# Feed-forward blocks that begin with k outermost over three weight units, on one core

## The chip, the cores and the metric

The kernel runs on one core of a Trainium2 chip. Its engines are TensorE (matrix products; PE, with its weight loads as PEld), VectorE (DVE), ScalarE (ACT) and SyncE (SP), which here only issues DMA transfers. GpSimd (POOL) does next to nothing. The metric is the device time of the one core in microseconds (us), lower is better. Times come from three runs; where time goes is read from one profiled execution.

## The reference

Two stacks of transformer layers work on one sequence of 256 tokens of width 1024, in float32. The first stack (2 layers) mixes with differential attention, SSD and GLA side by side; the second (4 layers) with stick-breaking, MoBA, sliding-window and again stick-breaking attention, each under a modulation (`ada`) by a condition vector. What the change touches is the feed-forward block that closes each of the six layers, and the end of the mixer ahead of it:

```python
# stack 1, layer i
h = h + mix @ w_out[i]
f = rms_norm(h, ffn_norm[i])
h = h + (jax.nn.silu(f @ w_ffn_gate[i]) * (f @ w_ffn_up[i])) @ w_ffn_down[i]

# stack 2, layer i
mod = c_act @ ada_w[i] + ada_b[i]
sh1, sc1, g1, sh2, sc2, g2 = [m[:, None, :] for m in jnp.split(mod, 6, axis=-1)]
...
x = x + g1 * y                                   # y: the attention's output
h = modulate(rms_norm_2(x, norm_gain[i, 1]), sh2, sc2)
x = x + g2 * swiglu(h, ffn_w_gate[i], ffn_w_up[i], ffn_w_down[i])
```

The hidden width of the feed-forward block is 2816.

## The kernel before, in words

**Layout.** x and h lie transposed in on-chip memory: 8 tiles of 128 features (k-tiles) by 256 tokens. All weights stream from memory once, in units of 128 x 1024 numbers (512 KB), one unit per buffer of `wslot`, slots 0 to 10. The attention phases use slots 0 to 3 (q, k, v, out projection), the GLA and SSD phases slots 0 to 7, the feed-forward blocks slots 8 (gate), 9 (up) and 10 (down), and slots 4 to 7 for the weights of a modulation table.

**Split products.** To keep float32 accuracy at the fast product rate, a weight unit is split in two: ScalarE copies it rounded into `w_hi` (helpers `mix_high` and `high`), VectorE writes the rest into `w_lo` (helpers `low_of` and `low`), and only then is the slot free for the next load. `w_hi` and `w_lo` have five parts; the attention uses parts 0, 1 and 4. h is split in the same way into `h_hi` and `h_lo`. A product is three matmuls (`three`: hi x hi, hi x lo, lo x hi) of 128 x 128 weights by 256 tokens, lines 575, 576 and 577 in turn.

**The phases.** `schedule` writes a list of phases: norm, attention (`att`), `ssd`, `gla`, `add`, `ffn` and so on. Every engine walks the same list in its own instruction stream, and the streams meet only at semaphores; `schedule` counts for each semaphore how often it has risen when a phase begins. Each engine does its instructions strictly in the order of the program.

**The feed-forward block (`ffn`).** It has 22 chunks (NF) of 128 hidden features. For one chunk TensorE does `up` (8 k-tiles of gate, then 8 of up: 48 matmuls into one bank), ScalarE silu, VectorE the product `mid`, both split mid, and TensorE does `down` (24 matmuls into `acc`). The order on TensorE is up(0), up(1), down(0), up(2), down(1) and so on, so that the elementwise work of a chunk lies under the next chunk's `up`. In one chunk's step VectorE does: the two `w_lo` of the next chunk, mid, the `w_lo` of down, mid_lo, and then, where the block carries a modulation table (`ada`), two `ada_unit` of two operations each. Four of the six blocks carry one: both of stack 1, and the first two of stack 2.

**Its beginning.** SP issues the loads of chunk 0's gate and up in the norm phase; slots 8 and 9 are free by then, so these go out as soon as SP gets there, behind the last out-projection unit of the attention. ScalarE splits them at the head of the norm phase, ahead of the squares, and VectorE ahead of its wait for `rstd`. After `rstd` VectorE makes the scaled tiles and, two tiles behind, `h_lo` (`h_low`), ScalarE `h_hi` between; the semaphore `h_parts` counts finished k-tiles. TensorE's `up(0, 0, first=True)` waits for `h_parts` ahead of each k-tile of gate. Chunk 1's units go through slots 8 and 9 too, after chunk 0's have been split.

**The last head of an attention phase.** `whole` is one step of the attention loop: on ScalarE and VectorE it handles pair of heads `i` and ends `prior = i - 1`. While there are more pairs, ScalarE (lines 1087 to 1091) and VectorE (`next_low`, line 1326) also split the q and k units of the next pair; in the last pair (`more` false) they don't. In stick-breaking attention `next_low` stands ahead of VectorE's reading of the scores (line 1353), in the others behind `qk_ready` and ahead of the same reading (line 1383).

## Time and profile before

| | us |
|---|---|
| median of 3 runs | 2578.78 |
| lowest, highest | 2577.83, 2583.71 |
| span of the profiled execution | 2580.4 |

The profiled execution's span, from its first instruction to its last, is 1.6 us above the median of the runs; nothing of note lies around it. The profile page gives busy time per engine, the groups of instructions by source line, and each group's mean duration. The trace behind it gives single instructions with their start, their duration, how long their engine had been idle before them and what ended that (in brackets), the chain of waits that leads to the last instruction, the busy time and the granted TensorE clock of any stretch (1.00 is 2.4 GHz, 0.50 is 1.2 GHz), and for each DMA the time from issue to landing. All starts are in us from the span's start. A matmul's own duration includes its way through the array; what counts for throughput is the distance from one start to the next.

### The profile page before, as it was taken

How to read it: one execution, taken by the hardware profiler on the slowest of the kernel's cores; microseconds unless marked ns; L12 is line 12 of the kernel's file. 1: busy time of each engine (PE TensorE's matmuls, PEld its weight loads, DVE VectorE, ACT ScalarE, POOL GpSimd, SP SyncE). 2: the span in 40 equal slices, each digit the busy share in tenths (PEclk: the TensorE clock that was granted, in tenths of full speed). 3: DMA queues.
4: the chain of work that ended last, by engine and by line, in shares of the span. 5: the costliest groups of instructions: out<-in, count | busy, mean ns of one | idle time of the engine just before them, and what ended most of it. 6: DMA issues, size and time to landing. Idle time of an engine off the chain costs nothing.

```text
span 2580.4 us, 44727 instructions
## 1 busy us (share of the span) xinstructions
PE 2369.4 (92%) x17136; PEld 2203.8 (85%) x17136; DVE 1498.5 (58%) x2564; ACT 1021.1 (40%) x1670; POOL 0.2 (0%) x4
## 2 busy tenths in 40 slices
PE   5799899988798899989899999899978899998998
PEld 4687699987686799979899978799966799897998
DVE  4433177745441477836677776577766554666544
ACT  3312244414231344325544444444444544455443
POOL 0000000000000000000000000000000000000000
PEclk8898799998898899999899999899989899998999
DMA  4343179962433299844289854299842366442664
GB/s 127 91 112 102 33 251 289 290 192 83 123 83 99 77 291 292 271 127 129 85 273 291 289 165 127 86 292 286 276 114 82 115 181 185 127 132 85 194 186 131
DMA packets 553295, 436.26 MB, mean 169 GB/s; under 512 B 31824, under 2 KB 479352, under 8 KB 553080
## 3 DMA queue, kind: packets, MB, share of 16 engines
q1 hardware_dynamic: 549840, 431.35, 55.2%
q10 hardware_dynamic: 3368, 3.71, 0.5%
q8 instruction: 59, 0.97, 0.2%
q14 instruction: 28, 0.23, 0.0%
HBM read 433.96 MB, written 1.05 MB: 169 GB/s over the span
## 4 chain that ended last, share of the span: by engine, by line
PE 85%; DVE 7%; ACT 3%; issue 1%; DMA 1%; DVEq 1%; ACTq 1%; SPq 0%
PE bank L575 12%; PE bank L576 12%; PE bank L577 12%; PE acc L575 6%; PE acc L576 6%; PE acc L577 6%; PE bank L561 5%; PE bank L702 5%; PE acc L620 3%; PE bank L980 2%; PE bank L779 2%; PE bank L585 1%; PE bank L570 1%; PE bank L691 1%; PE bank L745 1%
## 5 line engine op out<-in xcount | busy, mean ns | idle before, releaser
L575 PE MATMUL bank<-h_hi,w_hi 128*128 128x256 f32 x2704 | 787.4, 291 | 28.1 <-DVE h_lo L1251 16.1
L576 PE MATMUL bank<-h_lo,w_hi 128*128 128x256 f32 x2704 | 774.6, 286 | 0.0
L577 PE MATMUL bank<-h_hi,w_lo 128*128 128x256 f32 x2704 | 774.1, 286 | 0.0
L1013 ACT ACTIVATE w_hi<-wslot 128x1024 fp32r<-128x1024 f32 x510 | 529.8, 1054 | 527.9 <-PE acc L577 312.6
L1429 DVE TENSOR_TENSOR w_lo<-wslot,w_hi 128x1024 fp32r<-128x1024 f32 x396 | 473.2, 1221 | 263.0 <-ACT w_hi L1013 262.8
L575 PEld LDWEIGHTS bank<-h_hi,w_hi 128*128 128x128 f32 x2704 | 527.9, 195 | 46.9 <-issue 31.9
L576 PEld LDWEIGHTS bank<-h_lo,w_hi 128*128 128x128 f32 x2704 | 529.9, 196 | 0.0
L577 PEld LDWEIGHTS bank<-h_hi,w_lo 128*128 128x128 f32 x2704 | 528.8, 196 | 0.0
L575 PE MATMUL acc<-mid_hi,w_hi 128*128 128x256 f32 x1056 | 302.2, 286 | 0.5 <-DVE mid_lo L1662 0.5
L577 PE MATMUL acc<-mid_hi,w_lo 128*128 128x256 f32 x1056 | 298.7, 283 | 0.0
L576 PE MATMUL acc<-mid_lo,w_hi 128*128 128x256 f32 x1056 | 298.7, 283 | 0.0
L1251 DVE SCALAR_TENSOR_TENSOR head_work<-wslot,c_act,head_work 128x512 f32<-128x512 f32 x288 | 216.5, 752 | 24.0
L575 PEld LDWEIGHTS acc<-mid_hi,w_hi 128*128 128x128 f32 x1056 | 202.4, 192 | 0.8 <-DVE w_lo L1429 0.8
L576 PEld LDWEIGHTS acc<-mid_lo,w_hi 128*128 128x128 f32 x1056 | 202.6, 192 | 0.0
L577 PEld LDWEIGHTS acc<-mid_hi,w_lo 128*128 128x128 f32 x1056 | 202.4, 192 | 0.0
L1269 DVE TENSOR_TENSOR w_lo<-wslot,w_hi 128x1024 fp32r<-128x1024 f32 x114 | 136.2, 1220 | 49.8 <-ACT w_hi L1013 49.6
L561 PE MATMUL bank<-hT,wslot 128*128 128x256 f32 x640 | 143.1, 381 | 0.6 <-DVE sqT L1551 0.5
L702 PEld LDWEIGHTS bank<-wslot,hT 128*128 128x128 f32 x1088 | 129.2, 194 | 9.1 <-issue 9.1
L561 PEld LDWEIGHTS bank<-hT,wslot 128*128 128x128 f32 x640 | 120.9, 191 | 18.3 <-issue 1.5
L702 PE MATMUL bank<-wslot,hT 128*128 128x128 f32 x1088 | 136.2, 279 | 0.0
L575 PE MATMUL acc<-y_hi,w_hi 128*128 128x256 f32 x320 | 107.0, 334 | 21.1 <-DVE y_lo L1314 21.1
L1220 ACT ACTIVATE silu_g<-bank 128x256 f32<-128x256 f32 x132 | 49.7, 377 | 137.5 <-PE bank L577 137.3
(255 smaller groups left out, 2742.9 us busy)
## 6 DMA issues: line engine op xcount, KB each, us to landing
wslot<-in_ada_w_dram SPq DMA_DIRECT2D x192, 512.0 KB, 5.8
wslot<-in_ffn_w_gate_dram SPq DMA_DIRECT2D x88, 512.0 KB, 4.7
wslot<-in_ffn_w_up_dram SPq DMA_DIRECT2D x88, 512.0 KB, 5.4
wslot<-in_ffn_w_down_dram SPq DMA_DIRECT2D x88, 512.0 KB, 3.4
wslot<-in_w_in_dram SPq DMA_DIRECT2D x72, 512.0 KB, 4.0
wslot<-in_sb_w_in_dram SPq DMA_DIRECT2D x48, 512.0 KB, 4.5
wslot<-in_w_ffn_gate_dram SPq DMA_DIRECT2D x44, 512.0 KB, 4.9
wslot<-in_w_ffn_up_dram SPq DMA_DIRECT2D x44, 512.0 KB, 5.6
```

The costliest lines, as they stand in the source:

```text
L561: mm = pe.matmul(dst, wk(n, k), hT[:, k, :], start=(k == 0), stop=(k == KT - 1))
L575: pe.matmul(dst, w_hi[:, w, cols], hi, start=start, stop=False, skip_group_check=True)
L576: pe.matmul(dst, w_hi[:, w, cols], lo, start=False, stop=False, skip_group_check=True)
L577: return pe.matmul(dst, w_lo[:, w, cols], hi, start=False, stop=stop, skip_group_check=True)
L620: mm = pe.matmul(acc[:, m, :], wk(n, m), y, start=False, stop=False, skip_group_check=True)
L702: mm = pe.matmul(B(1, 256 + P * t, 384 + P * t), hT[:, k, P * t:P * t + P], wk(2, k), start=(k == 0), stop=(k == KT - 1))
L779: mm = pe.matmul(B(0, 0, 256), C("ones"), sqT[:, k, :], start=(k == 0), stop=(k == KT - 1))
L980: mm = pe.matmul(B(2 * b, 0, 256), wk(s, k), xT[:, k, :], start=(k == 0), stop=(k == KT - 1))
L1013: return act.activation(dst, src, ACT.Copy)
L1251: return dve.scalar_tensor_tensor(out=out, in0=x, scalar=scalar, in1=y, op0=op0, op1=op1)
L1269: dve.tensor_tensor(w_lo[:, part, :], wslot[:, n, :], w_hi[:, part, :], ALU.subtract)\
L1429: dve.tensor_tensor(w_lo[:, part, :], wslot[:, n, :], w_hi[:, part, :], ALU.subtract).then_inc(slot_used[n], 1)
```

## The change

**Loads.** The first unit of gate and up (slots 8 and 9) is no longer loaded in the norm phase but at the end of the phase ahead of it: in the second `gla` group of stack 1, and in the last pair of an attention phase of stack 2 (`first_units`). With them goes the gate unit of chunk 1, through slot 0. The up unit of chunk 1 goes through slot 1, from the norm phase. Chunk 2 is then the first one to be loaded into slots 8 and 9 in the block itself.

**Splits.** Three units (gate 0 to part 0, up 0 to part 1, gate 1 to part 2) are split in the phase ahead: in the last pair of heads, gate 0 and up 0 take the place where the next pair's q and k would be split, and gate 1 follows the last out-projection unit. In GLA all three stand at the phase's end. The norm phase splits one unit, up 1, into part 3. The first chunk's step in the block has no split of a next chunk any more. The differential attention of stack 1 is as it was.

**Products.** `first_two` does chunks 0 and 1: for each k-tile, once `h_parts` has it, the three matmuls of gate 0, up 0 and gate 1; then the 24 of up 1. `two_chunks(0, None)` no longer does `up(1)`. The same 96 matmuls are done in another order.

The core of the diff:

```diff
@@ schedule
         if split == "ffn":
-            counts.update(w_high=2, **slots(SLOT_FF, [1, 1]))
+            counts.update(w_high=1, **slots(SLOT_MIX + 1, [1]))
...
@@ SP
+            def first_units(stack, l, used, mix_used):
+
+                wg, wu, _ = ffn_weights(stack, l)
+                for n, w in enumerate((wg, wu)):
+                    load(SLOT_FF + n, mix_slot(SLOT_FF + n), unit(w, KT, 0), used[n] + 1)
+                load(0, mix_slot(0), unit(wg, KT, P), mix_used + 1)
...
                 if kind == "norm" and ph["split"] == "ffn":
-                    for n, w in enumerate(ffn_weights(ph)[:2]):
-                        load(SLOT_FF + n, mix_slot(SLOT_FF + n), unit(w, KT, 0), u[SLOT_FF + n] + 1)
+                    _, wu, _ = ffn_weights(ph["stack"], ph["layer"])
+                    load(1, mix_slot(1), unit(wu, KT, P), u[1] + 1)
...
                         if not more:
                             load(3, wslot[:, 3, :], wo[P * lo:P * lo + P, :], lo + u[3] + 1)
+                            if ph["att"] != "da":
+                                first_units(2, ph["layer"], u[SLOT_FF:SLOT_FF + 2], u[0] + ph["n"])
@@ TensorE
+                    def first_two():
+
+                        for s in (SLOT_FF, SLOT_FF + 1, 0):
+                            pe.wait_ge(slot_used[s], g(f"slot{s}") + 1)
+                        for k in range(KT):
+                            pe.wait_ge(sem["h_parts"], g("h_parts") - KT + k + 1)
+                            up_part(0, 0, k, k == 0)
+                            mm = up_part(0, 1, k, False)
+                            if k == KT - 1:
+                                mm.then_inc(sem["up_done"], 1)
+                            up_part(1, 0, k, k == 0)
+                        pe.wait_ge(slot_used[1], g("slot1") + 1)
+                        for k in range(KT):
+                            mm = up_part(1, 1, k, k == 0)
                         mm.then_inc(sem["up_done"], 1)
@@ ScalarE, attention
                         mix_high(0, 0, mix_full(0, i + 1))
                         if new_kv:
                             mix_high(1, 1, mix_full(1, ki + 1))
+                    elif i is not None and att != "da":
+                        for c in range(2):
+                            high(SLOT_FF + c, c, 16 * (g(f"slot{SLOT_FF + c}") + 1))
...
                     mix_high(3, PART_DOWN, mix_full(3, i))
+                    if not more and att != "da":
+                        high(0, 2, mix_full(0, ph["n"]))
@@ ScalarE, norm
                     if ph["split"] == "ffn":
-                        for n in range(2):
-                            high(SLOT_FF + n, n, 16 * (g(f"slot{SLOT_FF + n}") + 1))
+                        high(1, 3, 16 * (g("slot1") + g("extra1") + 1))
@@ VectorE, attention
                     def next_low():
+                        if not more:
+                            for c in range(2 if att != "da" else 0):
+                                low(SLOT_FF + c, c, g("w_high") + c + 1)
+                            return
...
                         mix_low(3, PART_DOWN, prior)
+                        if i is None and att != "da":
+                            low(0, 2, g("w_high") + 3)
...
                     if att == "sb":
-                        if more:
-                            next_low()
+                        next_low()
@@ VectorE, gla
+                    if gr:
+                        for n, part in ((SLOT_FF, 0), (SLOT_FF + 1, 1), (0, 2)):
+                            low(n, part, g("w_high") + part + 1)
```

What it moves, at the places that matter. The line numbers of the two kernels differ: 1013, 1269, 1429 and 1353 before are 1054, 1318, 1324 and 1412 after.

VectorE, the last pair of heads of the first stick-breaking layer, before. The scores are read in the second row.

```order
L1314 TENSOR_TENSOR y_lo<-bank,y_hi 128x256 [waits y_high]
L1353 TENSOR_SCALAR head_work<-bank 128x384 [waits scores] x2
L1356 TENSOR_SCALAR sm<-head_work 128x384 x2
L1360 TENSOR_TENSOR sm<-sm,pr 128x384 [waits sb_log]
```

After:

```order
L1368 TENSOR_TENSOR y_lo<-bank,y_hi 128x256 [waits y_high]
L1324 TENSOR_TENSOR w_lo<-wslot,w_hi 128x1024 [waits w_high] x2
L1412 TENSOR_SCALAR head_work<-bank 128x384 [waits scores] x2
L1415 TENSOR_SCALAR sm<-head_work 128x384 x2
L1419 TENSOR_TENSOR sm<-sm,pr 128x384 [waits sb_log]
```

Two subtractions now stand ahead of the reading, and each waits for ScalarE's `w_high`.

VectorE at the start of the first feed-forward block of stack 2, from the last pieces of h_lo to the split of chunk 2's units, before:

```order
L1251 SCALAR_TENSOR_TENSOR h_lo<-sqT,mod,h_hi 128x256 [waits h_high] x3
L1429 TENSOR_TENSOR w_lo<-wslot,w_hi 128x1024 [waits w_high] x2
L1659 TENSOR_TENSOR mid<-silu_g,bank 128x256 [waits silu_ready]
L1429 TENSOR_TENSOR w_lo<-wslot,w_hi 128x1024 [waits w_high]
L1662 TENSOR_TENSOR mid_lo<-mid,mid_hi 128x256 [waits mid_high]
L1412 TENSOR_SCALAR head_work<-wslot,c_act 128x512 [waits slot_full4]
```

After, to the same point and on to the split of chunk 2:

```order
L1300 SCALAR_TENSOR_TENSOR h_lo<-sqT,mod,h_hi 128x256 [waits h_high] x3
L1714 TENSOR_TENSOR mid<-silu_g,bank 128x256 [waits silu_ready]
L1324 TENSOR_TENSOR w_lo<-wslot,w_hi 128x1024 [waits w_high]
L1717 TENSOR_TENSOR mid_lo<-mid,mid_hi 128x256 [waits mid_high]
L1470 TENSOR_SCALAR head_work<-wslot,c_act 128x512 [waits slot_full4]
L1300 SCALAR_TENSOR_TENSOR head_work<-wslot,c_act,head_work 128x512
L1300 SCALAR_TENSOR_TENSOR head_work<-wslot,c_act,head_work 128x512 [waits slot_full5]
L1300 SCALAR_TENSOR_TENSOR head_work<-wslot,c_act,head_work 128x512
L1324 TENSOR_TENSOR w_lo<-wslot,w_hi 128x1024 [waits w_high] x2
```

Chunk 1's pair of subtractions is gone from between h_lo and mid; chunk 2's pair stays behind the ada work.

SP at the end of the first stick-breaking layer, after: the second to fourth of these loads are the first units, and the loads behind them follow without a wait for work that is still to be done.

```order
L425 DMA wslot<-in_sb_w_out_dram 128x1024 [waits slot_used3]
L425 DMA wslot<-in_ffn_w_gate_dram 128x8x128 [waits slot_used8]
L425 DMA wslot<-in_ffn_w_up_dram 128x8x128 [waits slot_used9]
L425 DMA wslot<-in_ffn_w_gate_dram 128x8x128 [waits slot_used0]
L425 DMA wslot<-in_ffn_w_up_dram 128x8x128 [waits slot_used1]
L425 DMA wslot<-in_ffn_w_down_dram 128x1024 [waits slot_used10]
L425 DMA wslot<-in_ada_w_dram 128x2x512 [waits slot_used4]
```

Before, this list went from the third row straight to a wait for slot 8, which VectorE frees in the norm phase.

## Rows read from the trace of the kernel before

**Rows 1.** The page: busy us, share, count; a group's count, busy, mean ns

```profile
PE 2369.4 (92%) x17136; PEld 2203.8 (85%) x17136; DVE 1498.5 (58%) x2564; ACT 1021.1 (40%) x1670; POOL 0.2 (0%) x4
...
L1013 ACT ACTIVATE w_hi<-wslot 128x1024 fp32r<-128x1024 f32 x510 | 529.8, 1054 | 527.9 <-PE acc L577 312.6
```

**Rows 2.** Chain of waits: start us, us to the next, what; three places

```profile
1284.97 0.21 PE acc L577
...
1294.99 0.40 DVE h_lo L1251
1295.38 0.40 DVE sqT L1251
...
1302.01 0.12 PE bank L576
```

**Rows 3.** Stretches of block starts: start:end, us, PE busy (matmuls), PEclk, DMA share, GB/s

```profile
333.09:346.47 13.38, 13.38 (x96) 0.88 0.77 249
886.50:901.01 14.51, 14.51 (x96) 0.79 0.75 234
1295.53:1309.29 13.76, 13.68 (x96) 0.88 0.73 235
1668.82:1683.19 14.37, 13.91 (x96) 0.88 0.63 212
...
sum 84.14, PE 83.07; mean PE 13.84
```

**Rows 4.** TensorE in order of time: first product of two blocks [idle before <-releaser]

```profile
1295.53 0.55 PE L575 MATMUL bank<-h_hi,w_hi 128*128 128x256 f32 x1 [1.88 <-DVE h_lo L1251]
...
1668.82 0.35 PE L575 MATMUL bank<-h_hi,w_hi 128*128 128x256 f32 x1 [1.89 <-DVE h_lo L1251]
```

**Rows 5.** Last heads of the first stick-breaking layer, VectorE and ScalarE in order of time

```profile
1271.96 1.02 DVE L1353 TENSOR_SCALAR head_work<-bank 128x384 f32<-128x384 f32 x2 [4.80 <-PE bank L657]
1272.55 0.52 ACT L1023 ACTIVATE pr<-head_work 128x384 f32<-128x384 f32 x1 [3.87 <-DVE head_work L1353]
...
1281.44 1.22 DVE L1269 TENSOR_TENSOR w_lo<-wslot,w_hi 128x1024 fp32r<-128x1024 f32 x1
...
1283.63 0.42 DVE L1314 TENSOR_TENSOR y_lo<-bank,y_hi 128x256 fp32r<-128x256 f32 x1 [0.97 <-ACT y_hi L1013]
```

**Rows 6.** First chunk of stack 2's first block: silu, mid_lo, chunk 2's gate split

```profile
1303.73 0.38 ACT L1220 ACTIVATE silu_g<-bank 128x256 f32<-128x256 f32 x1 [0.92 <-PE bank L577]
...
1306.23 0.42 DVE L1662 TENSOR_TENSOR mid_lo<-mid,mid_hi 128x256 fp32r<-128x256 f32 x1
...
1309.66 1.22 DVE L1429 TENSOR_TENSOR w_lo<-wslot,w_hi 128x1024 fp32r<-128x1024 f32 x1
```

**Rows 7.** Issue of up 0; landing us of up loads at 1267.33, 1292.44, 2386.29; all of wslot

```profile
1267.33 0.58 SPq L416 DMA_DIRECT2D wslot<-in_ffn_w_up_dram  x1
...
wslot<-in_ffn_w_up_dram SPq DMA_DIRECT2D x1, 512.0 KB, 6.1
...
wslot<-in_ffn_w_up_dram SPq DMA_DIRECT2D x1, 512.0 KB, 5.6
...
wslot<-in_ffn_w_up_dram SPq DMA_DIRECT2D x1, 512.0 KB, 4.9
...
DMA to landing us min/median/max: 3.2/5.0/15.7
```

**Rows 8.** Sliding-window layer, last heads: issue of up 0, VectorE's first reading of scores

```profile
1994.30 0.58 SPq L416 DMA_DIRECT2D wslot<-in_ffn_w_up_dram  x1
...
2000.69 0.56 DVE L1251 SCALAR_TENSOR_TENSOR sm<-bank,const 128x384 f32<-128x384 f32 x1 [2.69 <-PE bank L660]
```

**Rows 9.** MoBA layer, last heads: the same two

```profile
1633.40 0.58 SPq L416 DMA_DIRECT2D wslot<-in_ffn_w_up_dram  x1
...
1642.74 0.56 DVE L1251 SCALAR_TENSOR_TENSOR sm<-bank,const 128x384 f32<-128x384 f32 x1 [2.24 <-PE bank L660]
```

**Rows 10.** First stack, VectorE at the end of GLA, in order of time

```profile
324.29 0.69 DVE L1642 TENSOR_TENSOR xT<-xT,acc 128x512 f32<-128x512 f32 x1 [7.51 <-PE acc L620]
```

## What I predict, and how

> **What bounds the kernel now.** I read the page first: TensorE is busy for 92% of the span [rows 1]. So the time is the sum of TensorE's products and of the places where TensorE has none. Inside a feed-forward block, past its start, nothing else counts: products follow each other every 0.12 us at the full clock, and every 0.21 us at half of it [rows 2]. What is left to win or lose lies at two joints, and they are where the change works.
>
> The first is the start of the six feed-forward blocks. There h arrives from VectorE in eight k-tiles, one each 0.79 us (a 0.40 us piece of h_lo, then 0.40 us of scaling) [rows 2], and TensorE has three products per tile, 0.36 us of work at the full clock. From a block's first product to the first one of its down projection (96 products, chunks 0 and 1) the six take 84.14 us together, 13.38 to 14.51 each [rows 3]; the two that have no row there repeat rows that have one (the third stack-2 block 14.36, clock 0.88, like the second; the fourth 13.76, like the first). At 0.12 us a product 96 would need 11.5. TensorE stood idle 1.88 us ahead of such a start, waiting for h_lo [rows 4].
>
> The second joint is the end of an attention phase of stack 2. The last head's scores leave TensorE with nothing, and the chain runs over VectorE and ScalarE: in the first stick-breaking layer VectorE waits 4.80 us for the scores, and starts the moment they are there; ScalarE waits 3.87 us for VectorE [rows 5]. These holes look free, but each ends exactly when the chain goes on.
>
> **Part 1, k outermost: a gain.** With three units ready, each k-tile feeds nine products, 1.08 us at the full clock against a tile each 0.79 us. TensorE waits for the first tile only. Chunks 0 and 1 then need 96 x 0.12 + 0.13 (the first product's extra) = 11.65 us. While the granted clock is at its half level a product takes 0.213 us, so h us of half clock cost h x (1 - 0.12/0.213) = 0.44 h. Before, the granted means of 0.88 and 0.79 stand for (1 - mean) x 2 x length = 3.2, 6.1, 3.3, 3.45, 3.45 and 3.3 us at 1.2 GHz [rows 3]. In the first and third of these TensorE had been idle before the start and the half stretch began with it; I keep 3.2 and 3.3 (the fourth of stack 2 likewise), and cut the second one's 6.1 to 3.2, since TensorE was underfed through it. In the second and third block of stack 2 the first product ran at the full level (0.35 us against 0.55 [rows 4]) and the clock fell only during the trickle; with no trickle I take no half stretch there. Sum after: 2 x 13.05 + 2 x 13.1 + 2 x 11.65 = 75.6, a gain of **8.6 us**. Bounds: half stretches as long as before, 79.9 (gain 4.3); none, 69.9 (gain 14.2).
>
> The rule of the Trainium skill for this is in "TensorE: Matmul & The Clock Gate", section "HAM oscillation — how this bites in real kernels": run all k-tiles on end rather than wait between them, so that the array stays at its full clock. Taken at its word it gives the 14.2, the second rival below; the rows say that the idle ahead of the start is left as it is.
>
> **Part 2, the start's other end: a new stop.** Before, when chunk 0's gate and up were done, TensorE still had chunk 1's 48 products (5.76 us) to cover silu, mid and the split of down. Now 27 are left (3.24 us). From the start of silu to the end of mid_lo it took 1306.65 - 1303.73 = 2.92 us [rows 6]: just covered, I give 0.1 us a block, 0.5 in all (0 to 1). But in the four blocks with a modulation table to sum (both of stack 1, the first two of stack 2) VectorE then works through two ada units and only afterwards through chunk 2's gate split, whose first half ended at 1310.88, 7.15 us after silu's start [rows 6]. TensorE gets there after 3.24 - 0.2 + 24 x 0.12 = 5.9 us. It stops 7.2 - 5.9 = **1.3 us**, four times: 5.2 us. (The lower bound is 0.6 each, if ScalarE's earlier split lets VectorE close up, the upper 1.6.) After that a chunk has its 72 products again, 8.64 us, in which VectorE kept up before; it makes the debt good over the next chunks. In the two blocks without ada the split comes at once and costs nothing.
>
> **Part 3, the splits in the attention tails: a loss.** In the last head ScalarE now splits gate 0 and up 0 between copying v and the log chain, and VectorE subtracts both ahead of reading the scores. Both queues run in order, so the scores wait behind them, and they wait for the transfers. Those are issued where they were: up 0 at 1267.33, landing 6.1 us later [rows 7], 1273.43. ScalarE 1.05 [rows 1], VectorE 1.22 [rows 5], hand-overs 0.1: 1275.8 against 1271.96 [rows 5], 3.8 us. Before, nothing was behind up 0 in the DMA queue; now there are six more loads. An up load with others right behind took 5.6 us, one without 4.9 [rows 7], so up to 0.7 comes on top; I take 0.4, 4.2 us. At the tail's end VectorE also subtracts unit 2 (1.22) in a gap of 0.97 [rows 5]: 0.25. Two stick-breaking layers: **8.9 us** (8.2 to 9.6).
>
> The sliding-window layer: up 0 issued at 1994.30 [rows 8], the same 6.1: 2000.4, through both engines 2002.8, against scores read at 2000.69 [rows 8]: 2.1, with the 0.4 **2.5** (2.1 to 2.8). MoBA: VectorE's hole is 2.24 us [rows 9], the two subtractions take 2.44, and its transfers, issued 9.3 us ahead of the read (1633.40 against 1642.74), have landed by then: 0.2, with ScalarE's third split 0.3 (0.1 to 0.5). In stack 1 the three splits stand in GLA's tail, where VectorE has 7.51 us idle under the 32 products of the out projection [rows 10]; three times 1.22 is 3.7: nothing. If that cover were gone it would be 3.7 twice.
>
> Gone from the norm: a w_hi/w_lo pair on each engine, and one more pair in the first chunk. VectorE waited for rstd after them, 0; the loads that SP now issues early free nothing that anyone waits for, 0.
>
> **Sum.** -8.6 + 5.2 + 0.5 + 8.9 + 2.5 + 0.3 = **+8.8 us**. The profiled execution (span 2580.4) would become 2589.2; against the median of the runs, 2578.8, that is **2587.6**. Ends: -14.2 + 2.4 + 0 + 10.4 = -1.4, and -4.3 + 6.4 + 1 + 12.9 = +16.0.
>
> **Rivals.**
> The splits fit into the hole (not slower). Price: the tails fall from 11.7 to 0.8, 2576.7. It decides at one point: up 0 must have landed by 1271.96 - 1.22 - 1.05 - 0.1 = 1269.6, 2.3 us after its issue. The shortest landing of any load into wslot is 3.2 [rows 7]. For it: the hole itself is wider (4.80) than the work (2.44).
> The clock stays full in all six starts: 5.6 more, 2582.0. Against it: four of six starts began at half clock, after an idle that stays.
> VectorE catches up before TensorE asks for chunk 2: no 5.2, 2582.4. Against it: its order ada, then split is unchanged.
> All that is open goes badly (loads slowed by those behind, half clock as before): 2594.8.
>
> **Chances.** Forecast 0.50, fit 0.08, full clock 0.14, no stop 0.08, badly 0.13, others 0.07. A measurement of this kernel tells about 0.2%, 5.2 us, from no change. Slower: 0.44 of the forecast, all of "badly", 0.06 of the rest: 0.63. Within: 0.06, 0.04, 0.11, 0.06, 0.02: 0.29. Faster: 0.08, from the fit with a fuller clock and from what I don't see. The range for 8 in 10 takes the full clock and nearly all of the bad case, and leaves the fit: 2577.5 to 2594.
>
> **What would show it.** In the trace after: the six stretches from first product to first down product sum to some 76 us, with 96 products each and no wait for h_lo but the first; in four of them a TensorE idle of 1.3 us "w_lo" ahead of chunk 2; at the end of the stick-breaking layers a VectorE wait for ScalarE's w_hi, and of ScalarE for the DMA of ffn_w_up, with the scores read 4 us late; 2.5 us in sliding-window, next to none in MoBA and none in GLA. It is wrong if the scores are read on time, or if the clock turns out to be worth more than its 5.6 us: in the tails, above all, where it falls too and where I leave it at zero net.

## The result, and the profile after

| | before | changed |
|---|---|---|
| median, us | 2578.78 (5 runs) | 2589.59 (5 runs) |
| lowest, highest | 2577.26, 2583.71 | 2587.98, 2598.20 |
| span of the profiled execution | 2580.4 | 2587.7 |
| ratio, 95% interval | | 1.0046 [1.0027, 1.0065] |

The changed kernel is slower by 0.46%, some 12 us by the ratio. Its run of 2589.59 us has a span of 2587.7, so a run's time is its span and 1.9 us more. The profiled execution of before was then one of about 2582.3 us, in the upper part of the runs, and not 1.6 us above their median as I wrote ahead.

**The six starts.** From first product to first down product, as in [rows 3] (start:end, length, TensorE's busy time and matmuls, granted clock, DMA share, GB/s):

```profile
331.14:345.46 14.32, 14.31 (x96) 0.79 0.00 1
884.11:898.43 14.32, 14.32 (x97) 0.79 0.00 1
1300.29:1313.22 12.93, 12.93 (x97) 0.89 0.00 1
1673.30:1684.91 11.61, 11.61 (x96) 1.00 0.01 1
2031.48:2043.10 11.62, 11.62 (x97) 1.00 0.00 0
2385.50:2398.51 13.01, 13.01 (x96) 0.88 0.00 0
sum 77.81, PE 77.80; mean PE 12.97
```

Busy time equals length: TensorE no longer waits for h after the first tile. The MoBA and the sliding-window block run at the full clock and take 11.6 us, as worked out. Both stack-1 blocks have 0.79, that is 6.1 us at 1.2 GHz. The DMA share, 0.45 to 0.77 before, is nothing: those loads went out earlier.

**The stop ahead of chunk 2**, first block of stack 2, VectorE and then TensorE in order of time [idle before <-releaser]:

```profile
1310.56 0.42 DVE L1714 TENSOR_TENSOR mid<-silu_g,bank 128x256 f32<-128x256 f32 x1 [5.67 <-ACT silu_g L1269]
1311.51 1.23 DVE L1324 TENSOR_TENSOR w_lo<-wslot,w_hi 128x1024 fp32r<-128x1024 f32 x1 [0.52 <-ACT w_hi L1054]
...
1313.73 2.42 DVE L1300 SCALAR_TENSOR_TENSOR head_work<-wslot,c_act,head_work 128x512 f32<-128x512 f32 x3
1316.07 2.35 DVE L1324 TENSOR_TENSOR w_lo<-wslot,w_hi 128x1024 fp32r<-128x1024 f32 x2
```

```profile
1317.34 0.39 PE L597 MATMUL bank<-h_hi,w_hi 128*128 128x256 f32 x1 [1.02 <-DVE w_lo L1324]
```

The ada work (head_work) stands ahead of chunk 2's splits, and TensorE waits for the first of them. From the first down product (1313.22) to this row it takes 4.12 us, in all four blocks with a modulation table; before, it took 2.88 in every block. From here to their last product the four blocks take 184.9, 184.5, 184.5 and 184.5 us, against 184.4 before: the stop is paid once, and neither grows nor shrinks.

**The tail of the first stick-breaking layer**, the counterpart of [rows 5], VectorE:

```profile
1267.46 0.42 DVE L1368 TENSOR_TENSOR y_lo<-bank,y_hi 128x256 fp32r<-128x256 f32 x1 [0.29 <-ACT y_hi L1054]
1273.40 1.23 DVE L1324 TENSOR_TENSOR w_lo<-wslot,w_hi 128x1024 fp32r<-128x1024 f32 x1 [5.52 <-ACT w_hi L1054]
1275.75 1.22 DVE L1324 TENSOR_TENSOR w_lo<-wslot,w_hi 128x1024 fp32r<-128x1024 f32 x1 [1.12 <-ACT w_hi L1054]
1276.89 1.01 DVE L1412 TENSOR_SCALAR head_work<-bank 128x384 f32<-128x384 f32 x2
```

ScalarE beside it:

```profile
1272.31 1.06 ACT L1054 ACTIVATE w_hi<-wslot 128x1024 fp32r<-128x1024 f32 x1 [2.90 <-DMA wslot<-in_ffn_w_gate_dram]
1274.66 1.06 ACT L1054 ACTIVATE w_hi<-wslot 128x1024 fp32r<-128x1024 f32 x1 [1.29 <-DMA wslot<-in_ffn_w_up_dram]
```

SP's issue of up 0, and the landing of that transfer (last number, us):

```profile
1268.07 0.58 SPq L425 DMA_DIRECT2D wslot<-in_ffn_w_up_dram  x1
```

```profile
wslot<-in_ffn_w_up_dram SPq DMA_DIRECT2D x1, 512.0 KB, 6.6
```

The chain reads as one: up 0 is issued at 1268.07 and lands some 6.6 us later, ScalarE starts on it at 1274.66, VectorE follows at 1275.75, and only then, at 1276.89, reads scores that had long been there (no wait stands on that row). In [rows 5] the same reading waited for TensorE alone. It now comes 9.43 us after the y_lo ahead of it. In the trace of before that y_lo started at 1266.73, which makes 5.23:

```profile
1266.73 0.42 DVE L1314 TENSOR_TENSOR y_lo<-bank,y_hi 128x256 fp32r<-128x256 f32 x1 [0.30 <-ACT y_hi L1013]
```

In the sliding-window layer the two subtractions come at 2000.65 and 2002.97, and the scores are read at 2004.19, 6.99 us after y_lo at 1997.20, where it was 4.55:

```profile
2002.97 1.23 DVE L1324 TENSOR_TENSOR w_lo<-wslot,w_hi 128x1024 fp32r<-128x1024 f32 x1 [1.10 <-ACT w_hi L1054]
...
2004.19 0.55 DVE L1300 SCALAR_TENSOR_TENSOR sm<-bank,const 128x384 f32<-128x384 f32 x1
```

### The profile page after: what moved, and what is told of

Same layout as the page of the kernel before. It is cut to its first block, busy times and chain, and to the rows that moved or that the text cites. A ratio compares the mean times of both kernels' runs of the same rounds, so it can differ in the third digit from the quotient of the medians.

```text
span 2587.7 us, 44670 instructions
## 1 busy us (share of the span) xinstructions
PE 2360.2 (91%) x17136; PEld 2197.3 (85%) x17136; DVE 1496.9 (58%) x2564; ACT 1020.9 (39%) x1670; POOL 0.2 (0%) x4
## 4 chain that ended last, share of the span: by engine, by line
PE 82%; DVE 8%; ACT 4%; DMA 2%; DVEq 1%; issue 1%; ACTq 1%; SPq 0%
PE bank L597 12%; PE bank L598 12%; PE bank L599 12%; PE acc L597 6%; PE acc L598 6%; PE acc L599 6%; PE bank L583 5%; PE bank L724 4%; PE acc L642 3%; PE bank L1021 2%; PE bank L801 2%; PE bank L607 1%; PE bank L592 1%; DVE head_work L1300 1%; DVE w_lo L1324 1%
## 5 line engine op out<-in xcount | busy, mean ns | idle before, releaser
L1054 ACT ACTIVATE w_hi<-wslot 128x1024 fp32r<-128x1024 f32 x510 | 529.9, 1054 | 529.1 <-PE acc L599 314.0
```

The costliest lines, as they stand in the source:

```text
L1054: return act.activation(dst, src, ACT.Copy)
```

## The experiments

All are timed against runs of the kernel before on the same chip, and the ratios are taken that way. The theory: three terms make the result, a gain at the starts (k outermost), a stop ahead of chunk 2 (ada work first), and late scores in the tails (splits that wait for transfers). The rivals: the stop only moves debt that comes back later; the tails are late for another reason than the transfers; two units would have been enough.

**Chunk 2's splits first.** In the first chunk's step VectorE splits chunk 2's units ahead of the ada units, not behind (`next_pair` makes the same two `low` calls).

```diff
-                        if more and not first:
-                            for n, what in enumerate(("gate", "up")):
-                                low(SLOT_FF + n, 2 * (1 - b) + n, count + split_index(what, f + 1))
...
+                        if more and not second and not first:
+                            next_pair(f, b)
...
+                        if first:
+                            next_pair(1, 1)
                         if ada is not None:
```

> The changed kernel, with one thing moved: in the first chunk's step of a feed-forward block VectorE subtracts chunk 2's gate and up units ahead of the two ada units, not behind them. Theory (TensorE's stop ahead of chunk 2 is VectorE's order): the 4.12 us from the first down product to chunk 2's first product in the four ada blocks falls to 2.9, 5.0 us less in all, 2584.6 against the changed kernel's 2589.6. Rival (VectorE has too much to do in these blocks, and the wait comes back one chunk later): 2589.6.

Measured: 2585.59 us, ratio 1.0027 [1.0016, 1.0038].

```profile
1306.12 2.35 DVE L1324 TENSOR_TENSOR w_lo<-wslot,w_hi 128x1024 fp32r<-128x1024 f32 x2
1308.57 0.49 DVE L1470 TENSOR_SCALAR head_work<-wslot,c_act 128x512 f32<-128x512 f32 x1
```

The splits now come first. The distance from first down product to chunk 2 falls from 4.12 to 2.95 us in all four blocks, and the rest of each block keeps its length (184.4 to 184.7 us). So the stop is the order on VectorE, and no debt is behind it.

**Loads first.** The changed kernel, with SP's loads of gate 0 and up 0 at the start of the attention phase of stack 2, where slots 8 and 9 have long been free. The splits stay.

```diff
+                    if ph["att"] != "da":
+                        first_pair(2, ph["layer"], u[SLOT_FF:SLOT_FF + 2])
...
-                                first_units(2, ph["layer"], u[SLOT_FF:SLOT_FF + 2], u[0] + ph["n"])
+                                third_unit(2, ph["layer"], u[0] + ph["n"])
```

> The changed kernel, with one thing moved: in the attention phases of stack 2 SP issues the loads of gate 0 and up 0 at the phase's start, where slots 8 and 9 are free already, and not behind the last out-projection unit. The splits stay in the last pair of heads. Theory (the tails lose to transfers that two in-order queues wait for): VectorE's 2.44 us of subtractions fit into its hole of 4.80, the scores of both stick-breaking layers are read 4 us earlier, those of sliding-window 2.4, in all some 10.5 us less: 2579. Rival (it is the splits' own work on both engines that delays the chain, wherever the data are): 2589, with the scores read as late as now.

Measured: 2584.32 us, ratio 1.0011 [1.0001, 1.0021]. The same tail, VectorE:

```profile
1269.37 0.43 DVE L1373 TENSOR_TENSOR y_lo<-bank,y_hi 128x256 fp32r<-128x256 f32 x1 [0.30 <-ACT y_hi L1059]
1272.30 2.36 DVE L1329 TENSOR_TENSOR w_lo<-wslot,w_hi 128x1024 fp32r<-128x1024 f32 x2 [2.50 <-ACT w_hi L1059]
1274.63 1.02 DVE L1417 TENSOR_SCALAR head_work<-bank 128x384 f32<-128x384 f32 x2
```

The same two subtractions, in the same place, now fit into the hole: the scores are read 5.26 us after y_lo, against 5.23 before the change. The splits were never the loss; the transfers they waited for were. In the sliding-window layer the scores are read 5.77 us after y_lo here and 4.55 in the version with both repairs, as before the change; VectorE then waits for TensorE, not for a split. The ratio falls by 0.0035, some 9 us of the 10.5 expected, and such a difference is known to about 0.002.

**Both.**

> Both edits together, the split of chunk 2 ahead of the ada units and the early loads. Theory: the two stops are apart in time and add up, 15.5 us less than the changed kernel, 2574, that is 0.2% faster than the kernel before; what is left of the change is k outermost's 6.3 us, less 0.8 in the tails. Rival (one stop stands for the other, or the clock takes the gain back): 2579 or more.

Measured: 2576.26 us, ratio 0.9990 [0.9981, 0.9999]. The starts:

```profile
330.95:343.97 13.02, 13.02 (x97) 0.88 0.00 1
884.38:898.69 14.31, 14.31 (x96) 0.79 0.00 1
...
2021.33:2035.51 14.18, 14.18 (x96) 0.79 0.00 0
...
sum 79.15, PE 79.15; mean PE 13.19
```

With both repairs the change is worth a little, 0.1%, at the edge of what can be told. Of the 8.6 us forecast for the starts 5.0 remain in this trace. The sliding-window block, at the full clock in the trace of the changed kernel, is at half clock for 5.8 us here, with nothing changed at its start.

**Two units.** The kernel before, with k outermost over gate 0 and up 0 alone; loads, splits and tails as before.

```diff
-                    up(0, 0, first=True)
...
+                    for k in range(KT):
+                        pe.wait_ge(sem["h_parts"], g("h_parts") - KT + k + 1)
+                        for n in range(2):
+                            mm = three(B(0, 256 * n, 256 * n + 256), n, k_cols(k), h_hi[:, k, :], h_lo[:, k, :],
+                                       k == 0 and n == 0, k == KT - 1)
+                    mm.then_inc(sem["up_done"], 1)
```

> The kernel before, with k outermost over two units only: chunk 0's gate and up, six products for each k-tile. Loads and splits as before. Theory (a third unit is needed, since chunk 1's split comes late): TensorE is through with chunk 0 by 6.1 us after its first product, but VectorE has gate 1's split at 7.6, so it stops 1.5 us, and first product to first down product takes 13.4 us a block; in all 3 us less than before, 2576. Rival (two units do as well, 11.9 us a block): 2567.

Measured: 2580.43 us, ratio 1.0006 [0.9994, 1.0018].

```profile
1660.98:1674.48 13.50, 12.14 (x96) 1.00 0.64 213
2019.47:2032.98 13.51, 12.14 (x96) 1.00 0.42 133
...
sum 83.32, PE 80.35; mean PE 13.39
```

At the full clock 13.50 us, as expected (13.4), of which TensorE is busy 12.14. Six products per tile, 0.72 us, don't quite cover the 0.79 that a tile takes, which costs 0.5 us. The rest is one stop, between chunk 0 and chunk 1, for VectorE's split of gate 1:

```profile
1668.62 0.39 PE L575 MATMUL bank<-h_hi,w_hi 128*128 128x256 f32 x1 [1.36 <-DVE w_lo L1436]
```

It has no cost in the tails, and no gain that can be told: the 2576 us expected did not come. The third unit, split ahead of the block, is what makes the start dense.

**The old order of products** in the changed kernel: its loads and splits stay, gate 0, up 0, gate 1 and up 1 are done one after the other.

```diff
                             up_part(0, 0, k, k == 0)
-                            mm = up_part(0, 1, k, False)
-                            if k == KT - 1:
-                                mm.then_inc(sem["up_done"], 1)
+                        for k in range(KT):
+                            mm = up_part(0, 1, k, k == 0)
+                        mm.then_inc(sem["up_done"], 1)
+                        for k in range(KT):
                             up_part(1, 0, k, k == 0)
```

> The changed kernel with its early loads and splits kept and only the products put back in the old order: gate 0 (which takes the eight waits for a part of h), up 0, gate 1, up 1, each over its own eight k. Theory: k outermost gave 6.3 us over the six starts and took 5.0 us back as the stop ahead of chunk 2, since it ends chunks 0 and 1 some 2 us sooner and leaves VectorE as much less time for the splits of chunk 2. So without it the six stretches grow by 6.3 us together (towards 14.0 each at a mixed clock), the stop falls from 4.12 to 2.9 us, and the sum is the changed kernel plus 1.3 us: 2590.9 us. Rival: the stop hangs on the update units on VectorE alone and stays with the old order; then both are paid, and the time is 2589.6 + 6.3 = 2595.9 us. Second rival: the six stretches keep their gain from the early splits alone, and the time is 2589.6 - 5.0 = 2584.6 us.

Measured: 2593.36 us, ratio 1.0052 [1.0032, 1.0072].

```profile
334.10:348.60 14.50, 14.50 (x96) 0.79 0.13 45
...
1676.24:1690.59 14.35, 13.90 (x96) 0.88 0.13 45
...
sum 84.89, PE 84.14; mean PE 14.02
```

The starts are back at 84.9 us, and the distance ahead of chunk 2 at 2.88 in all six blocks. So k outermost and the stop come together, and the trace shows how. VectorE ends chunk 2's first split 7.14 us after silu's start in every block with a table, whatever the order of products. What changes is when silu starts: chunk 0's sums are complete after 48 of the 96 products in the old order and after 69 with k outermost, so silu starts 5.56 us ahead of the first down product in the old order, here and in the kernel before, and 3.07 us ahead of it in the changed kernel. Against the changed kernel's two ratios the product order is worth nothing to 0.0006 (1.3 to 3.8 us by the medians), which these runs can't tell from nothing. What is left, 0.5% over the kernel before, are the tails. In this trace's last layer up 0 took 8.3 us to land, and the tail was 2.2 us longer than in the changed kernel:

```profile
wslot<-in_ffn_w_up_dram SPq DMA_DIRECT2D x1, 512.0 KB, 8.3
```

**Matmuls on constants in the wait.** Ten matmuls of 128 columns behind the clearing of acc in each norm ahead of a feed-forward block, into a bank that nobody reads, in the changed kernel and in the version with both repairs.

```diff
                     mm.then_inc(sem["sumsq"], 1)
                     clear_acc()
+                    if ph["split"] == "ffn":
+                        for _ in range(10):
+                            pe.matmul(B(3, 0, 128), C("ones"), C("ones"), start=True, stop=True)
```

> The changed kernel with ten matmuls of 128 columns on constants, into a bank nobody reads, put on TensorE behind the clearing of acc in the norm ahead of each feed-forward block: they fill some 1.1 of the 1.8 us in which TensorE otherwise waits for the first part of h. Nothing waits for them but the products behind. Theory: the half clock in these starts (6.14 us in both stack-1 blocks, 2.97 and 3.20 in the stick-breaking ones, none in the other two) comes from this wait. Filled, the stretches from the first product to the first down product fall from 14.31, 14.31, 12.93 and 13.02 to about 11.6 us, 8.2 us in all: 2581.4 us. Rival: the level follows from what lies further back, and the stretches stay as they are: 2589.6 us, or up to 2 us more where the added matmuls run at half clock and hold the first product back.

> The version with the loads of gate 0 and up 0 ahead of the attention phase and the splits of chunk 2 ahead of the update units (2576.3 us), and with the ten added matmuls of the run before. Theory of the wait: its stretches of 13.02, 14.31, 12.92, 11.62, 14.18 and 13.11 us all become about 11.6, 9.5 us in all: 2566.8 us, the fastest kernel of the study. Rival (the level is set further back): 2576.3 us.

Measured: 2595.85 us, ratio 1.0065 [1.0048, 1.0082], and with both repairs 2576.04 us, 0.9986 [0.9973, 1.0000]. TensorE in the first, and its starts:

```profile
1299.50 1.03 PE L632 MATMUL acc<-zero 1*128 1x512 bf16 x4
1300.46 2.50 PE L806 MATMUL bank<-const 128*128 128x128 f32 x20
1302.71 0.37 PE L597 MATMUL bank<-h_hi,w_hi 128*128 128x256 f32 x1
```

```profile
334.45:346.08 11.63, 11.63 (x100) 1.00 0.01 1
...
2394.53:2406.15 11.62, 11.62 (x100) 1.00 0.00 0
sum 69.73, PE 69.73; mean PE 11.62
```

A matmul in plain float32 leaves two records here (the norm's 8 are listed as 16). The ten take 2.25 us, from 1300.46 to 1302.71, twice what I had reckoned, and so hold the first product back. All six starts are at 2.4 GHz for their whole length, in both kernels: the half clock in the starts does come from TensorE's wait ahead of them. That half of the theory held. The other half, that the time follows, did not: 2595.9 us instead of 2581.4, and 2576.0 instead of 2566.8.

**The changed kernel and the added matmuls once more, on one chip.**

> The changed kernel itself, once more, as the partner of the next run on the same chip. It gives a second trace of the same program, so that the spread of the granted clock outside the six block starts can be told from an effect of the edits. Expected 2589 to 2592 us. The distances that don't hang on the clock (4.12 us ahead of chunk 2 in the update blocks, 9.4 us from the last y_lo but one to the reading of the scores) should come back within 0.1 us; the time at half clock outside the starts may differ by 10 us or more from the first trace (the first trace shows 81.9 us of it in the first mixing phase, other kernels' traces 75 to 92 us in that same, unchanged stretch).

> The changed kernel with the ten added matmuls ahead of each feed-forward block, once more, beside the changed kernel on one chip. Its first run was 2595.9 us although its trace shows all six starts at full clock: 8.1 us less from first product to first down product, 2.1 us more ahead of the first product (0.37 us in the first, 6.77 for 6.40 us from the norm's first product). Theory: the added matmuls are worth nothing, since what the starts gain comes back as half clock or as delay in other stretches: the difference to the run beside it is between 0 and +6 us. Rival: the slower first result was chance, and the trace's own sum holds: 6 us faster than the run beside it.

Measured: 2592.09 us, ratio 1.0052 [1.0036, 1.0068], and 2591.13 us, 1.0045 [1.0032, 1.0058]. The two ratios differ by 0.0007, less than their intervals: 6 us of gain (0.0023) are not excluded by this pair alone, but the first pair points the other way, and the pair with both repairs shows nothing. In the second trace of the changed kernel the 4.12 us ahead of chunk 2 came back to 0.01 us. The 9.4 us to the reading of the scores did not, against what was expected: it is 10.0 us in the first stick-breaking layer, where up 0 landed in 7.1 us instead of 6.6. And its starts are other ones than in the first trace, from the same program:

```profile
333.64:346.67 13.03, 13.03 (x97) 0.88 0.00 1
883.71:898.01 14.30, 14.30 (x97) 0.79 0.01 1
1300.22:1314.46 14.24, 14.24 (x96) 0.79 0.00 1
...
2034.33:2048.48 14.15, 14.15 (x97) 0.80 0.00 0
...
sum 80.29, PE 80.28; mean PE 13.38
```

What did the added matmuls cost? From the end of the first h_lo to the first product it takes 0.45 to 0.51 us in five of the six starts, where it took 0.15, and 0.16 in the sliding-window block: 1.6 us in all. And in both their runs gate 0 lands later in the stick-breaking tails (6.0 to 6.8 us after its issue, against 4.7 to 4.9 in the traces of the changed kernel, of the splits first and of the old order), and each of these tails is 1.2 to 1.9 us longer than in the changed kernel. ScalarE in the first of these tails, where [2.90] stood:

```profile
1274.75 1.06 ACT L1057 ACTIVATE w_hi<-wslot 128x1024 fp32r<-128x1024 f32 x1 [5.05 <-DMA wslot<-in_ffn_w_gate_dram]
```

Beside each late landing of gate 0 there is a transfer of another kind: one packet of 16 KB of the program's own instructions, on queue q8. In this tail it starts at 1267.32, 0.56 us ahead of gate 0's issue, and takes 0.88 us; the DMA view of 1267.2:1267.8 shows it alone:

```profile
q8 instruction: 1, 0.02, 9.1%
```

Over the four attention tails of all twelve traces gate 0 (in the versions with early loads: the gate unit issued in its place) took 4.6 to 5.0 us in the 39 cases with no such packet under way between its issue and its landing, and 6.0 to 6.8 us in eight of the nine with one; in the ninth it took 5.0. All nine are in kernels with added matmuls, which load 60 such packets and not 59. That the added instructions moved these packets onto the transfer, and that this delays it, is the reading that fits; no run moved them alone, so it is not shown. Nor is gate 0 needed for a tail so long: two of the eight stick-breaking tails without added matmuls took 27.7 and 28.6 us, with gate 0 on time and up 0 landing in 7.3 and 8.3 us.

Where the loads go out early there is nothing to lengthen, and there the added matmuls cost nothing that can be told.

**Third unit's split behind y_lo**, in the version with both repairs.

```diff
                         mix_low(3, PART_DOWN, prior)
-                        if i is None and att != "da":
-                            low(0, 2, g("w_high") + 3)
...
                         out_low(prior)
+                        if i is None:
+                            low(0, 2, g("w_high") + 3)
```

> The same version without added matmuls, and with VectorE's split of the third unit (gate of chunk 1) behind the subtraction of y for the last unit instead of ahead of it. It should take 0.25 us out of the path in each stick-breaking layer and nothing elsewhere, as VectorE waits after that subtraction anyway: 2575.8 us, which can't be told from 2576.3 by time; the trace shows it in the distance from the split to the last y_lo. Rival: the split then holds back the sum into the residual and the norm, and the time is the same or up to 2 us longer.

Measured: 2576.19 us, ratio 0.9989 [0.9976, 1.0002]. It can't be told from its parent, nor was it expected to be. The last y_lo starts 0.42 us after its y_hi, against 0.49: 0.07 us are gained there and not 0.25, and the tail of the first stick-breaking layer has the same 22.2 us with and without.

## Right or wrong, point by point

The measured time lies within the forecast range, 2 us above the forecast. By the terms, each read in the two traces of the changed kernel against the one of before:

| term | forecast, us | first trace | second trace |
|---|---|---|---|
| six starts, k outermost | -8.6 | -6.3 | -3.9 |
| stop ahead of chunk 2, four blocks | +5.2 | +5.0 | +5.0 |
| wait for mid_lo | +0.5 | +0.1 | +0.1 |
| two stick-breaking tails | +8.9 | +8.0 | +8.3 |
| sliding-window tail | +2.5 | +2.9 | +2.8 |
| MoBA tail | +0.3 | -0.1 | 0.0 |
| sum | +8.8 | +9.6 | +12.3 |
| the span itself | +8.8 | +7.3 | +10.3 |

Most of what the sum has too much, 2.3 and 2.0 us, lies in the mixing phases outside the tails, which are 3.4 and 2.7 us shorter than in the trace of before.

A tail is here the distance from the last y_lo but one to the norm's first product: 22.3, 23.0, 22.9 and 22.4 us before, 26.4, 22.9, 25.7 and 26.3 after.

**Part 1 was mis-sized.** The mechanism is as told: nine products a tile, no wait but the first. What failed is the step that gave each block a half stretch: I cut the second block's from 6.1 to 3.2 us, since TensorE would no longer be underfed, and left the first block's at 3.2. Both showed 6.14, and 3.0 us of half clock more cost 1.3 us each: the 2.3 us that the first trace lacks. The second trace has 3.2 and 6.1 us there, but 6.0 in the first stick-breaking block, where I had 3.3, and 5.8 in the sliding-window block, where I had none. In six traces of kernels with this start and no added matmuls the sum is 77.8, 77.8, 79.2, 79.2, 79.2 and 80.3, and never 75.6; the half clock in a block start comes as 0, about 3 or about 6 us, and not in the same places in the two traces of the same program. The rival "clock full in all starts" (2582.0) was made to happen, by added matmuls, and its time did not come. The Trainium skill ("TensorE: Matmul & The Clock Gate", section "HAM oscillation — how this bites in real kernels") advises to run all k-tiles on end so that TensorE stays at its full clock. Here that gave a full clock in two of the six starts in the first trace and in one in the second; in the others the half clock follows the wait ahead of the start, which it leaves, and with that wait filled it was gone from all six.

**Part 2 was right**, the stop to 0.06 us (1.24 against 1.3), its cause (27 products of cover instead of 48, and ada work ahead of the split), and that only the blocks with ada work have it. "VectorE catches up" is refuted by the rows.

**Part 3 was right** in its way and its size: the scores are read 4.2 us late in the first stick-breaking layer (9.43 - 5.23), 3.8 in the last, 2.4 in the sliding-window layer, not at all in MoBA (5.14 us after y_lo in both kernels); in the second trace 4.8, 3.9 and 2.3. In the first GLA tail VectorE still waits 3.67 us for TensorE after the three splits, so they cost nothing there. The third unit's split at the end of a tail, taken as 0.25 us, cost 0.1. The landing of up 0, reckoned as 6.1 with 0.4 on top, was 6.6 and 7.1 us in the first layer's two traces and 6.2 in the last layer's first. That "fit" failed for the reason given: not the length of the splits, but when up 0 lands.

**What the sum left out** is the clock in the tails, which I named as a place where I could be wrong. TensorE in the last 30 us ahead of the norm, in the first and the last stick-breaking layer, before:

```profile
1259.07:1289.07 30.00, 23.01 (x152) 0.77 0.20 53
2341.07:2371.07 30.00, 23.01 (x151) 0.77 0.20 54
```

Changed:

```profile
1263.82:1293.82 30.00, 18.75 (x121) 0.72 0.60 176
2349.04:2379.04 30.00, 19.14 (x122) 0.72 0.53 141
```

With the loads first:

```profile
1261.89:1291.89 30.00, 22.94 (x150) 0.77 0.46 141
2344.41:2374.41 30.00, 22.94 (x151) 0.77 0.38 106
```

0.77 is 13.7 us at 1.2 GHz, 0.72 is 17.1. All six traces in which the scores are read on time (before, two units, loads first, and the three with both repairs) have 13.7 in both places, all six with late scores 16.2 to 17.1, whatever their starts. The longer wait thus takes about 3 us more of half clock with it, twice. Part of it lies in the wait itself, where it costs nothing.

That the clock weighs in the total can be read from the runs alone, since each has its span and its mean granted clock. In 68 runs of the kernel before the times go from 2571.4 us at a mean of 0.943 to 2589.9 at 0.933, and a line through them falls by 1.44 us for each 0.001. With this slope for all kernels, each one's mean time at a mean clock of 0.938, and the mean clock that it had (single runs lie 1.7 us about the line, so these times are good to 0.3 us for the long series and to about 1 us for those of five or six runs):

| kernel | at 0.938, us | mean clock |
|---|---|---|
| before (three series) | 2580.8, 2580.2, 2580.8 | 0.9391, 0.9395, 0.9377 |
| changed (two series) | 2589.3, 2590.4 | 0.9364, 0.9358 |
| old order of products | 2589.0 | 0.9358 |
| splits first | 2583.6 | 0.9365 |
| loads first | 2582.2 | 0.9374 |
| two units | 2579.9 | 0.9377 |
| both, both with split behind y_lo | 2576.3, 2575.3 | 0.9382, 0.9382 |
| changed with added matmuls (two series) | 2594.6, 2596.4 | 0.9382, 0.9412 |
| both with added matmuls | 2576.8 | 0.9393 |

At the same clock the change costs 8.7 to 9.8 us, near the forecast's sum. The rest, up to the 12 to 13 us of the two ratios, goes with the mean clock, lower by 0.002 to 0.003 in each series of the changed kernel. The tails' 3 us, twice, would be 0.0012 of that; the rest of the difference is not placed. For the kernels with added matmuls this column is no fair comparison, since the edit itself raises the clock, in the starts, and the column takes that out again.

**What stays open**: why added matmuls that hold the starts at the full clock don't shorten the whole by what the starts gain. The later first product and the longer tails account for 5.3 of 8.1 us in the first pair of traces and 4.4 of 10.5 in the second. In the version with both repairs, whose tails can't lengthen, 9.4 us of shorter starts became a ratio lower by only 0.0004. Where the rest went can be seen in part. In all three pairs the mixing phases (tails included) are longer with added matmuls, by 11.2, 5.2 and 7.1 us, with 22, 7 and 13 us more at 1.2 GHz. The mean clock of the runs says the same for the first and the third pair: it rose by 0.0018, 0.0054 and 0.0011, where the half clock gone from the starts alone would raise it by 0.0036, 0.0046 and 0.0042. Whether the added matmuls bring half clock into later phases, or the draws fell so, these runs can't tell: two traces of the changed kernel itself differ by 7 us there.

## What to carry to other kernels

A hole in an engine's queue takes moved work only if that work's input is there when the hole opens: ask when the transfer was issued, not how long the work is. Here the same two splits cost 4.2 us behind late loads and nothing behind early ones. Where products are packed closer at one joint, see what the engine feeding the next joint has queued ahead; k outermost won 4 to 6 us and gave 5 back there. And a stretch of a few us at half clock in one trace can be a draw and not a property of the kernel (the same start had 6.1 us in one trace and 3.2 in the next): size a gain from it by several traces or by the runs' mean clock.

## What the runs showed of the hardware

The same program differs from run to run mainly by its granted clock: by the line above, 0.010 of mean clock go with 14 us in the kernel before. The length at 1.2 GHz in the first, unchanged mixing phase (some 297 us) was 75, 82, 89 or 92 us in different traces. The Trainium skill, in "TensorE: Matmul & The Clock Gate", section "What's actually happening", says that the number of matmuls at the low clock at a kernel's start varies from run to run of the same kernel. These traces show the same inside a kernel, with 3.2 or 6.1 us at half clock in the same block start.

A 512 KB load landed in 4.7 us with one load just ahead of it, and loads issued 0.5 and 1.1 us later in 6.6 and 9.1 us. Up 0, the second of these, landed in 6.0 to 6.1 us in the stick-breaking tails of the kernel before, with no load right behind it, and in 6.2 to 8.3 us over the six traces with several behind it; the loads behind are not the whole of that spread, since the same program gave 6.6 and 7.1 us in the same place.

A 16 KB packet of instructions, 0.9 to 1.4 us long, went with a landing later by 1 to 2 us in eight of the nine cases in which it fell between a load's issue and its landing: 6.0 to 6.8 us against 4.6 to 5.0 for the same load, as told above.
